# Delta-rule inverse in two halves of two heads, decay tables in two parts (layer 2 mixers, one core)

## The reference

```python
def gdn_mixer(qkv, z, b, a, conv_w, dt_bias, a_log, norm_w):
    ...
    gc = jnp.cumsum(g.reshape(bsz, nc, CHUNK, GDN_HEADS).transpose(0, 3, 1, 2), axis=-1)
    decay = lower_exp_diff(gc)
    kbeta = kc * betac[..., None]
    strict = jnp.tril(jnp.einsum('bhcid,bhcjd->bhcij', kbeta, kc) * decay, -1)
    rhs = jnp.concatenate([vc * betac[..., None], kbeta * jnp.exp(gc)[..., None]], axis=-1)
    sol = lax.linalg.triangular_solve(strict, rhs, left_side=True, lower=True, unit_diagonal=True)
    u, w = jnp.split(sol, [GDN_HEAD_V], axis=-1)
    qk = jnp.einsum('bhcid,bhcjd->bhcij', qc, kc) * decay

    def step(state, inp):
        q_i, k_i, u_i, w_i, qk_i, g_i = inp
        v_new = u_i - jnp.einsum('bhld,bhde->bhle', w_i, state)
        o = (jnp.einsum('bhld,bhde->bhle', q_i * jnp.exp(g_i)[..., None], state)
             + jnp.einsum('bhls,bhse->bhle', qk_i, v_new))
        ...
```

## Time and profile before

| | us |
|---|---|
| median of three runs | 2384.55 (2382.06 to 2385.46) |
| the profiled execution's own time | 2383.82 |
| its span, first to last instruction | 2382.0 |
| TensorE (PE) busy in the span | 2291.2 (96%) |
| VectorE (DVE) / ScalarE (ACT) / GpSimd (POOL) busy | 1544.9 / 946.9 / 317.3 |

### The profile page before, as it was taken

The page is one execution under the profiler, slowest core; times in us unless marked ns, Lnnn a source line. Parts: engine busy times, 40 slices in busy tenths (PEclk is TensorE's granted clock), DMA queues, the critical chain, the costliest instruction groups (busy, mean ns, idle before and its releaser), DMA issues. The chain is left out here.

```text
span 2382.0 us, 31843 instructions
## 1 busy us (share of the span) xinstructions
PE 2291.2 (96%) x11560; PEld 1910.7 (80%) x11560; DVE 1544.9 (65%) x2014; ACT 946.9 (40%) x1589; POOL 317.3 (13%) x305
## 2 busy tenths in 40 slices
PE   7999999999999999999999899988999999999997
PEld 6888888887788878787878788876887888888885
DVE  4555555465855446568788787764688777775557
ACT  4434343444333321343444455544333333334443
POOL 0111111121000000002232455440011000000000
PEclk9999999999999999999999899999999999999999
DMA  3111111110333364433332421203325343438654
GB/s 141 45 55 36 45 64 45 55 45 27 123 107 106 124 247 150 142 108 112 106 106 90 140 80 53 66 13 115 107 103 198 150 154 150 172 132 301 224 184 170
DMA packets 102618, 273.36 MB, mean 115 GB/s; under 512 B 9356, under 2 KB 35180, under 8 KB 98028
## 3 DMA queue, kind: packets, MB, share of 16 engines
q1 hardware_dynamic: 102508, 271.88, 32.9%
HBM read 196.03 MB, written 75.81 MB: 114 GB/s over the span
## 5 line engine op out<-in xcount | busy, mean ns | idle before, releaser
L94 PE MATMUL psG<-h_hi,w_hi 128*128 128x512 f32 (+1 forms) x880 | 224.8, 395 | 2.0 <-DVE features_T L1818 1.6
L94 PE MATMUL psG<-h_hi,w_lo 128*128 128x512 f32 (+1 forms) x880 | 223.2, 391 | 0.0
L94 PE MATMUL psG<-h_lo,w_hi 128*128 128x512 f32 (+1 forms) x880 | 222.6, 392 | 0.0
L94 PEld LDWEIGHTS psG<-h_hi,w_hi 128*128 128x128 f32 x880 | 159.5, 189 | 35.6 <-issue 3.0
L94 PEld LDWEIGHTS psG<-h_lo,w_hi 128*128 128x128 f32 x880 | 160.4, 189 | 30.6
L94 PEld LDWEIGHTS psG<-h_hi,w_lo 128*128 128x128 f32 x880 | 159.2, 188 | 30.0
L409 POOL TENSOR_TENSOR sb_w<-sb_left 128x128 f32<-128x128 f32 (+3 forms) x96 | 89.1, 931 | 470.1 <-DVE sb_left L552 464.1
L560 DVE TENSOR_TENSOR sb_w_lo<-psT,sb_w_hi 128x512 fp32r<-128x512 f32 (+1 forms) x80 | 50.7, 634 | 146.7 <-ACT sb_w_hi L434 146.7
L124 DVE TENSOR_TENSOR w_lo<-w_raw,w_hi 128x1024 fp32r<-128x1024 f32 x62 | 75.7, 1222 | 93.9 <-ACT w_hi L119 93.7
L426 ACT ACTIVATE sb_left<-psA 128x128 f32<-128x128 f32 (+3 forms) x96 | 47.1, 491 | 184.7 <-PE psA L694 113.5
L119 ACT CAST w_hi<-w_raw 128x1024 fp32r<-128x1024 f32 x64 | 67.3, 1051 | 126.1 <-PE psG L94 74.4
(11 more groups left out here) (608 smaller groups left out, 5724.4 us busy)
## 6 DMA issues: line engine op xcount, KB each, us to landing
w_raw<-in_units SPq DMA_DIRECT2D x100, 512.0 KB, 3.7
w_raw<-hidden_blocks SPq DMA_DIRECT2D x77, 256.0 KB, 2.9
merge_gates<-features_T SPq DMA_DIRECT2D x12, 1024.0 KB, 7.7
merge_gates<-merge_gates SPq DMA_DIRECT2D x12, 1024.0 KB, 4.8
features<-features_T SPq DMA_DIRECT2D x24, 512.0 KB, 3.8
w_spare<-in_units SPq DMA_DIRECT2D x22, 512.0 KB, 4.3
hidden_blocks<-features_T SPq DMA_DIRECT2D x11, 1024.0 KB, 3.9
down_sums<-w_spare SPq DMA_DIRECT2D x22, 512.0 KB, 3.3
```

The source lines that it names most:

```text
L94: return pe.matmul(out, lhs, rhs, start=first, stop=last, skip_group_check=True)
```

## The change

It does seven things.

1. Every level of the inverse runs as two halves, a (heads 0 and 1) and b (heads 2 and 3), each with its own steps. Half a writes bank 6 for both T and X, half b bank 5 (`own_bank`). The transposes of both halves still go to bank 7.
2. TensorE issues Ya, Ta, Yb, Tb, then later Xa, Xb. In front of Yb it waits for ScalarE's copy `VTa`, since Yb writes the bank that this copy reads.
3. ScalarE's and VectorE's copies and subtractions of 128 x 512 become two of 128 x 256.
4. `o` moves to the second half of bank 7 and `ds` to bank 5; T2b waits for `s3` of the tile before.
5. `tr1` moves ahead of T2, `level_t(64)` ahead of the transposes `ptr`, and on ScalarE `product(64)` ahead of `pt`.
6. The tables of decays: subtraction, clamp and exponential run in two parts, first the four GDN heads (`dsub0`, `dmask0`, `L0`), then the eight SSD heads (`dsub1`, `dmask1`, `L1`); the second clamp moves behind `sdif`, the second exponential behind `product(64)`.
7. VectorE's level 32 moves ahead of `nt` and `qkd`.

```diff
+        two = lambda g: slice(2 * g, 2 * g + 2)
+        own_bank = lambda g: PS[:, 6 - g, 0:2 * P]
...
                 def product(b):
-                    if b > 2:
-                        tensG.wait(a, f"Y{b // 2}", i)
-                        if b == 4:
-                            tensG.wait_last(a, "vn", i)
-                        scalG.done(f"VT{b // 2}", a.copy(VT[:].rearrange("p h t -> p (h t)"), bank(7)))
-                    tensG.wait(a, f"T{b}", i)
-                    tensG.wait_last(a, "X64", i) if b == 2 else tensG.wait(a, f"X{b // 2}", i)
-                    if b < 64:
-                        scalG.done(f"T{b}", a.copy(T1[:].rearrange("p h t -> p (h t)"), bank(5)))
...
+                    for g, k in enumerate("ab"):
+                        if b > 2:
+                            tensG.wait(a, f"Y{b // 2}{k}", i)
+                            if b == 4:
+                                tensG.wait_last(a, "vn", i)
+                            scalG.done(f"VT{b // 2}{k}", a.copy(VT[:, two(g)].rearrange("p h t -> p (h t)"), PS[:, 7, 2 * P * g:2 * P * g + 2 * P]))
+                        tensG.wait(a, f"T{b}{k}", i)
+                        if b < 64:
+                            scalG.done(f"T{b}{k}", a.copy(T1[:, two(g)].rearrange("p h t -> p (h t)"), own_bank(g)))
...
                 if front:
-                    vectF.wait(a, "dmask", n)
-                    scalF.done("L", a.activation(DEC[:], DEC[:], ACT.Exp))
+                    vectF.wait(a, "dmask0", n)
+                    scalF.done("L0", a.activation(DEC[:, SH:NH], DEC[:, SH:NH], ACT.Exp))
...
+                if chain:
+                    product(64)
+                if front:
+                    vectF.wait(a, "dmask1", n)
+                    scalF.done("L1", a.activation(DEC[:, 0:SH], DEC[:, 0:SH], ACT.Exp))
                     tensF.wait(a, "ptr", n)
                     tensF.wait_last(a, "att", n)
                     scalF.done("pt", a.copy(PTR[:].rearrange("p n t -> p (n t)"), bank(1, 2)))
-                if chain:
-                    product(64)
...
                 def level(b):
...
+                    for g, k in enumerate("ab"):
+                        tensG.wait(v, f"X{b}{k}", i)
+                        if b < 64:
+                            scalF.wait(v, "v1", i)
+                            vectG.done(f"V{b}{k}", tt(flat(V[:, two(g)]), flat((V0 if b == 2 else V)[:, two(g)]), own_bank(g), ALU.subtract))
...
                     vectF.done("sdif", tt(sdif[:], row("sinks", AH), mx[:], ALU.subtract))
-
-                    scalF.wait(v, "L", n)
+                    no_later(1)
+                level(32)
+                if front:
+                    scalF.wait(v, "L0", n)
...
                 def level_t(b):
...
                     poolF.wait(pe, f"nm{LEVELS.index(b)}", i)
+                    for g, k in enumerate("ab"):
+                        if b == 2:
+                            scalF.wait(pe, "v1", i)
+                            if g:
+                                vectG.wait_last(pe, "s3", i)
+                        else:
+                            vectG.wait(pe, f"V{b // 2}{k}", i)
+                            if g:
+                                scalG.wait(pe, f"VT{b // 2}a", i)
+                            elif b == 4:
+                                vectG.wait_last(pe, "og", i)
+                            for h in (2 * g, 2 * g + 1):
+                                x = pe.transpose(PS[:, 7, h * P:(h + 1) * P], V[:, h], C["ident"][:])
+                            tensG.done(f"Y{b // 2}{k}", x)
+                        for h in (2 * g, 2 * g + 1):
+                            at = h % 2 * P
...
+                                x = mm(own_bank(g)[:, at:at + P], NM[:, LEVELS.index(b), h], (V0 if b == 2 else V)[:, h])
+                        tensG.done(f"T{b}{k}", x)
...
-                level_t(2)
                 if front:
                     pe.wait_ge(f_here, 16 * n + 16)
                     vectF.wait_last(pe, "att", n)
                     turn(tensF, "tr1", 1, [F[:, c] for c in range(GQ0, GQ0 + 4)])
+                level_t(2)
...
                 level_x(32)
+                level_t(64)
                 if front:
                     for h in range(AH):
...
                     tensF.done("ptr", x)
-                level_t(64)
```

More of the change, by code:

```diff
@@ L2145, in layer2_mixers @@
         half = lambda h: slice(64 * (h % 2), 64 * (h % 2) + 64)
+        two = lambda g: slice(2 * g, 2 * g + 2)
+        own_bank = lambda g: PS[:, 6 - g, 0:2 * P]
         tensF = Steps(sem("tensor_front"), "tr1 tr2 tr3 tr4 tr0 sc swas gtk gtq qk ptr yo v1t att y stn")
-        tensG = Steps(sem("tensor_chain"), "T2 X2 Y2 T4 X4 mtrm Y4 T8 X8 Y8 T16 X16 Y16 T32 X32 Y32 T64 X64 wt vn o ds")
+        tensG = Steps(sem("tensor_chain"), "T2a T2b X2a X2b Y2a T4a Y2b T4b X4a X4b mtrm Y4a T8a Y4b T8b X8a X8b Y8a T16a Y8b T16b X16a X16b "
+                                           "Y16a T32a Y16b T32b X32a X32b Y32a T64a Y32b T64b X64a X64b wt vn o ds")
         tensH, scalH = Steps(sem("tensor_turned"), "mtrg"), Steps(sem("scalar_turned"), "mtg")
-        scalF = Steps(sem("scalar_front"), "qk sq vb z ga lnr expr xs L kt qt e0 e1 e2 e3 es pt v1")
-        scalG = Steps(sem("scalar_chain"), "T2 yq0 yq1 yln yexp VT2 T4 mtm VT4 T8 VT8 T16 VT16 T32 VT32 T64 wt vn osq oln oexp")
-        vectF = Steps(sem("vector_front"), "ss ssc nqk kb qg dsub dmask swab mx mx2 ngm sdif nt qkd m1 vt1 sd0 sd1 xdt xdec den rden "
+        scalF = Steps(sem("scalar_front"), "qk sq vb z ga lnr expr xs L0 kt qt e0 e1 e2 e3 es L1 pt v1")
+        scalG = Steps(sem("scalar_chain"), "T2a T2b yq0 yq1 yln yexp VT2a T4a VT2b T4b mtm VT4a T8a VT4b T8b VT8a T16a VT8b T16b "
+                                           "VT16a T32a VT16b T32b VT32a T64a VT32b T64b wt vn osq oln oexp")
+        vectF = Steps(sem("vector_front"), "ss ssc nqk kb qg dsub0 dsub1 dmask0 swab mx mx2 ngm sdif dmask1 nt qkd m1 vt1 sd0 sd1 xdt xdec den rden "
                                            "yo yx att st1 y yz st2")
-        vectG = Steps(sem("vector_chain"), "V2 ysc ym0 ym1 V4 V8 V16 V32 VT64 oss osc s0 s1 s2 s3 og ogz")
+        vectG = Steps(sem("vector_chain"), "V2a V2b ysc ym0 ym1 V4a V4b V8a V8b V16a V16b V32a V32b VT64a VT64b oss osc s0 s1 s2 s3 og ogz")
         poolF = Steps(sem("gpsimd_front"), "par keep0 keep1 xd kprev nm0 nm1 nm2 vbt nm3 nm4 nm5 vprev")
@@ L2370, in level, with less_own, no_later @@
                         return
[L2371 to L2376, removed]
+                    for g, k in enumerate("ab"):
[3 more added lines that the diff above has]
+                            vectG.done(f"V{b}{k}", tt(flat(V[:, two(g)]), flat((V0 if b == 2 else V)[:, two(g)]), own_bank(g), ALU.subtract))
+                        else:
+                            vectG.done(f"VT64{k}", tt(VT[0:64, two(g), 64:], VT[0:64, two(g), 64:], heads(own_bank(g)[0:64, :], 2)[:, :, 64:], ALU.subtract))
+                def less_own(m):
+                    hs = (slice(SH, NH), slice(0, SH))[m]
+                    vectF.done(f"dsub{m}", tt(DEC[:, hs], DEC[:, hs], per(PT[:, PACS + hs.start:PACS + hs.stop], hs.stop - hs.start, P), ALU.subtract))
+                def no_later(m):
+                    hs = (slice(SH, NH), slice(0, SH))[m]
+                    vectF.wait(v, f"dsub{m}", n)
+                    vectF.done(f"dmask{m}", v.scalar_tensor_tensor(DEC[:, hs], DEC[:, hs], 0.0, over(MSK[:, 0, :], hs.stop - hs.start), ALU.min, ALU.add))
                 level(2)
@@ L2410, in tile @@
                     v.wait_ge(dec_here, 16 * n + 16)
-                    vectF.done("dsub", tt(DEC[:], DEC[:], per(PT[:, PACS:PACS + NH], NH, P), ALU.subtract))
+                    less_own(0)
                 level(8)
                 if front:
-                    vectF.wait(v, "dsub", n)
-                    vectF.done("dmask", v.scalar_tensor_tensor(DEC[:], DEC[:], 0.0, over(MSK[:, 0, :], NH), ALU.min, ALU.add))
+                    less_own(1)
+                    no_later(0)
                     tensF.wait(v, "swas", n)
@@ L2446, in tile @@
                 if front:
-                    scalF.wait(v, "L", n)
+                    scalF.wait(v, "L1", n)
                     tensF.wait(v, "sc", n)
@@ L2658, in tile @@
                 if chain:
-                    vectG.wait(pe, "VT64", i)
+                    vectG.wait(pe, "VT64b", i)
                     poolG.wait(pe, "kbg", i)
```

65 lines of the change are left out of this document (25 added, 40 removed).

## The result

| | before | changed |
|---|---|---|
| median of 6 runs each | 2382.57 us (2381.36 to 2385.46) | 2394.55 us (2390.0 to 2397.05) |
| ratio | | 1.0048, 95% interval 1.0035 to 1.0061 |
| profiled execution, its span | 2382.0 us | 2392.7 us |
| mean granted clock over the span | 0.990 | 0.987 |
| Y at level 4, one tile to the next | 35.81 us | 37.02 to 39.73 us |

The changed kernel takes 12 us more (forecast: 9.4 over the 2382.57 of these runs, inside the range). Its page shows how little of that is work: VectorE and ScalarE have 64 and 96 instructions more and are busy for 17 and 15 us more, but TensorE has the same 11,560 matmuls and the span is 10.7 longer.

A forecast was written before the change was run, and what follows sets the result against it. TensorE was taken as the bound, busy 32.16 of 35 us. Seven tiles x (1.25 + 0.3) = +10.9, last tile -3.6, first front 0: +7.3 on 2383.82 gives 2391.1, median 0.7 above: 2392 us, range 2383 to 2402.

The forecast's parts named there:

- Level 4: Beside a front, Yb waits 2.13 us for ScalarE's copy VTa; TensorE is +0.44 us late after X.
- the walk: Step-by-step timing of TensorE through one tile beside a front, from 1447.10, ending +1.25 us late at `v1t`.
- Level 8: Beside a front, Yb waits 0.88 us for ScalarE's copy behind `mtg`; the tile is then +1.40 us late.
- Levels 16 to 64: Rest of the tile beside a front: +0.66 us at level 16, +1.07 at 32, +1.25 at `v1t`.
- The 17 waits and increments: Added on TensorE in each tile by the finer steps; taken as 0.3 us, between nothing and 1.0.
- The first front: Front running alone at the start: earlier `kt` against later L1 and T2, put at 0, between -1 and +1 us.
- The last tile: Chain alone: halves shorten levels; 2.7 + 0.6 + 0.5 us won, less 0.2 for added instructions: -3.6 us, once.
- rival A: Gaps at level 4 lower TensorE's clock, about 1.7 us per fall: 2404 in all tiles, 2396 likelier; chance 0.22.
- Rival B: Not slower: GpSimd's work shifts, VectorE delivers V2a up to 1.15 us sooner, 2381; half within same 0.22, rest within faster 0.12.
- Rival C: Yb finds VTa done at every level, so halves win: -24 us, 2361; only a trace within faster 0.12.

The follow-up runs named there:

- Own banks: Changed kernel with each half's transposes in the free half of its own bank 6 or 5, no wait for VTa between halves: 2368.88 us, ratio 0.9938.
- ScalarE's order: Changed kernel with ScalarE's level 4 copies ahead of yln, yexp, z, ga and level 8's ahead of mtg, mtm: 2372.97 us, ratio 0.9958.
- The move of level 8's copies alone: Changed kernel with only product(8) moved ahead of mtg and mtm on ScalarE: 2391.14 us, ratio 1.0033.
- the kernel with the filler: Changed kernel with 14 unread identity transposes ahead of TensorE's wait at level 4, in tiles with a front: 2388.85 us, ratio 1.0025.
- level 4's move alone: Changed kernel with only product(4) moved ahead of yln, yexp, z and ga on ScalarE: 2380.37 us, ratio 0.9988.
- the kernel with both remedies: Changed kernel with half transposes in their own banks and ScalarE's product(4) and product(8) early: 2367.81 us, ratio 0.9935.

## Why the prediction was right, and where its sizes were off

**Level 4** was forecast as a gap of 2.13 ended by ScalarE's `m_vt`. Measured from the same point it is 1.85 + 0.16 = 2.01, with that releaser. Shifted by 3.82, the walk puts Ya at 1455.32 (measured 1455.32), Yb at 1458.18 (1458.06) and `mtrg` at 1460.27 (1460.11). Own banks and ScalarE's order both take the gap away, each by its own end of the wait, and the loss goes with it: the mechanism is shown.

**Level 8** was forecast at 0.88 and measured at 0.89 + 0.16. Shifted, Yb was due at 1462.83 and stands at 1462.70. The move of level 8's copies alone removes it.

**Levels 16 to 64**: +1.25 forecast at `v1t`, 1479.11 shifted, measured 1479.07, so +1.21. The gap of 0.42 at level 32 is 0.36 + 0.16 = 0.52, and its releaser is the one named.

**The 17 waits and increments**, taken as 0.3 per tile, measured nothing: an undisturbed tile takes 37.02, the walk without them gave 37.06. This term was mis-sized by 2.1 us in all. The walk itself is off by up to 0.16 on the way, so a row is the better witness: with own banks, where no wait holds TensorE between the halves, Ya to `tr0` takes 1.39 (1483.61 to 1485.00), just what Y to `tr0` took in whole levels (1451.76 to 1453.15), with one more wait and two more increments in it. By the Trainium skill ("TensorE: Matmul & The Clock Gate", section "The cost: per-tile semaphore tail") increments at the ends of matmuls follow one another at about 26 ns each, which makes an estimate of 0.45 per tile. The traces do not agree: the two increments of that row cost less than 0.01.

**The first front**, put at 0 between -1 and +1, gave -2.2, of which -0.3 is an earlier start and -1.9 the front itself, outside its bounds. The prediction had L0 letting `kt` start 1 to 2 us sooner and set L1 and T2 against it; the first came in full, and the others took nothing back. TensorE starts the scores at 1326.70 behind a gap of 0.68, where it stood 3.44 until 1328.82; with the table in one part it starts them at 1328.14, and the 1.9 are gone.

**The last tile**, forecast at -3.6, gave -3.1 from T2. The clean levels are right: 3.61 for the one behind `mtg` and `mtm` (forecast -0.6, measured -0.57), then -1.29 twice (forecast -2.7 for both, measured -2.58). Level 4, "perhaps 0.5" less, was 0.31 more (5.74 against 5.43). Both have a fall of the clock there: before, Y and T of that level ran at it, and in the change X takes 1.79. In the kernel with the filler the last tile has none and goes from Ya at level 4 to Ya at level 8 in 4.69.

**The clock (rival A)** is the step that failed: the forecast held it at 1.00 beside the front. Rival A with two or three falls, 2396 and a part of its 0.22, is how the kernel runs. There are four falls beside a front in the profiled execution, of 1.44, 2.71, 1.64 and 1.28 us, against the 1.7 given for one; the longest ran at 0.50 for 6 us, where the prediction had counted on 3. Without a gap at level 4 there are none (level 4's move alone), with that gap filled there are none, and with that gap alone they come in every tile. The prediction had the row for it and gave it the smaller chance, since no row said whether gaps of 2.8 us were enough. What decides it stays open: two stretches of 3 us in the trace after, both with 0.88 busy, are followed by 1.00 in one tile and by 0.50 in the next. It fits the spread of the runs after: the run of 2390.0 has a mean granted clock of 0.990, the two of 2397.05 have 0.987 and 0.986. That this spread (7 us) is wider than the one before says little, for 4 us in the first six runs of the kernel before became 6 in 22. By the Trainium skill (the same page, Part 1, "The HAM clock gate") TensorE's recent activity is looked at in a window that runs freely, whatever the kernel does. By that a like gap could count in one tile and not in the next; the traces fit it, but no run here moved a gap in time by itself, so it is not shown.

**Rival B** (GpSimd's work falls elsewhere) came only in part and won nothing: `yz` takes the same 1.23, and while `osc` became 0.21 shorter, the decay of the SSD state ahead of it became 0.65 longer. That VectorE's work on operands in SBUF is held up by GpSimd was argued from the earlier trace rows and not tried. **Rival C** was right about what halves are worth once no half waits for the other's copy: own banks give a tile of 34.49.

The misses partly cancel: -2.2 for the first front and -2.1 for the waits against +7.4 for the falls and +0.8 for the last tile, +3.9 on top of the forecast's +7.3. So the direction and the size per tile rest on the mechanism; that the sum came within 3 us is luck.

## What to carry to other kernels

When a step is cut in two so that two engines overlap, look at what the second half waits for. If both halves use one buffer, the second waits for the other engine's copy of the first, and that copy comes when everything queued ahead of it on its engine is done; give each half its own bank, or move the copy to the front of that engine's list. Work that used to be issued ahead of a wait and now stands behind it is the price, and a gap on TensorE can be paid twice, once in waiting and once in a lower clock behind it.

## What the runs showed of the hardware

- A fall of the clock needs no single long pause: two gaps of 0.68 and 1.85 us with some 0.9 us of work between them were followed by a stretch at 0.50, 1.2 GHz, and a fall cost 1.3 to 2.7 us. Filling the second gap with 1.69 us of idle transposes kept 1.00 in every tile beside a front. In the first tile of the kernel with both remedies a single gap of 2.07 us was followed by a fall, while 2.59 us in the first tile of the change was not.
- With the same gap of 1.85 us at level 4 in every tile, a profiled execution had a fall in four of the six tiles behind the first (the change), in one of six (decays in one part) or in all six (level 8's copies moved alone). These are counts of one execution each, and the one with a single fall was the fastest of its five runs. What makes the difference stays open. Where they came in all (tile 37.56), the runs agreed within 1.0 us, so a narrow spread is no sign that the clock is whole.
- Seventeen more waits and increments per tile on TensorE, all on groups that are spaced out, cost nothing that the traces show: a tile of 37.02 against 37.06 without them in the sum, and 1.39 from Y to `tr0` with whole levels and with halves in banks of their own.
